# Expert rows gathered by a table from TensorE, outputs scattered to token order, and five places for expert weights in a hybrid encoder layer

## What is computed

```python
x1 = x + merged @ w_out
h = rmsnorm(x1, ffn_norm_g)
g_idx = argmax(h @ w_group_router + b_group_router)        # one of 4 groups, weight g_w
e_logit = (h @ w_expert_router + b_expert_router)[group g_idx]   # 8 experts
top_p, top_i = top_k(softmax(e_logit), 2)
expert_id = g_idx * 8 + top_i
hid = silu(h @ w_exp_gate[e]) * (h @ w_exp_up[e])          # 1024 -> 256
y = x1 + sum over the two chosen e of g_w * top_p[e] * (hid @ w_exp_down[e])
```

## Time and profile before

| | us |
|---|---|
| three runs | 1710.51, 1710.72, 1713.13 |
| median | 1710.72 |
| profiled run | 1707.65 |
| its span | 1706.0 |
| TensorE busy | 1521.2 (89%) |
| VectorE busy | 534.1 (31%) |
| DMA, mean over the span | 148 GB/s |

### The profile page before, as it was taken

How to read it: one execution, slowest core, us unless ns; L and a number is a source line. 1 busy time by engine, 2 the same in 40 slices (tenths; PEclk the granted TensorE clock), 3 DMA queues, 4 the chain that set the end, 5 groups by cost and what they waited for, 6 DMA issues and landing times.

```text
span 1706.0 us, 16754 instructions
## 1 busy us (share of the span) xinstructions
PE 1521.2 (89%) x6566; PEld 841.4 (49%) x6566; DVE 534.1 (31%) x1484; ACT 295.3 (17%) x682; POOL 120.9 (7%) x191
## 2 busy tenths in 40 slices
PE   5999999998799999978999999999999929787870
PEld 3554655445455544455555444765554615444440
DVE  2215598016300033442001344244661521010103
ACT  3224111223101011243000011434000201101100
POOL 6000000112000000000000100100000020000003
PEclk9999999999899999999999999999999859989886
DMA  7332345201521335143114140220132368999995
GB/s 200 126 85 84 94 154 122 82 18 50 156 79 49 123 107 189 50 148 149 50 49 148 50 129 1 75 87 25 50 107 107 120 262 336 422 422 421 422 392 197
DMA packets 132553, 253.15 MB, mean 148 GB/s; under 512 B 11136, under 2 KB 88960, under 8 KB 118144
## 3 DMA queue, kind: packets, MB, share of 16 engines
q1 hardware_dynamic: 115536, 183.55, 30.4%
q0 software_dynamic: 16944, 68.60, 11.2%
HBM read 214.21 MB, written 37.91 MB: 148 GB/s over the span
## 4 chain that ended last, share of the span: by engine, by line
PE 77%; DMA 13%; DVE 4%; issue 2%; ACT 2%; POOL 1%; SPq 1%; DVEq 0%; ACTq 0%; POOLq 0%
PE ps L679 18%; DMA arena<-slot_rows 10%; PE ps L698 7%; PE ps L600 7%; PE ps L610 6%; PE ps L1131 4%; PE ps L649 3%; PE ps L559 3%; PE ps L629 3%; PE ps L1195 2%; PE ps L601 2%; PE ps L611 2%; PE ps L699 2%; PE ps L721 1%; PE ps L1174 1%
## 5 line engine op out<-in xcount | busy, mean ns | idle before, releaser
L679 PE MATMUL ps<-bulk 128*128 128x512 f32 x688 | 303.4, 598 | 2.3 <-issue 2.3
L679 PEld LDWEIGHTS ps<-bulk 128*128 128x128 f32 x688 | 129.8, 192 | 155.8 <-issue 155.8
L600 PE MATMUL ps<-bulk 128*128 128x512 f32 x256 | 133.3, 603 | 4.1 <-DMA bulk<-in_w_in 4.1
L698 PE MATMUL ps<-bulk 128*128 128x512 f32 x256 | 135.2, 610 | 0.0
L610 PE MATMUL ps<-arena,bulk 128*128 128x512 f32 x256 | 131.2, 595 | 1.8 <-DVE arena L1739 1.8
L1174 PE MATMUL ps<-bulk,arena 128*64 128x256 f32 x1024 | 115.8, 385 | 5.4 <-DMA bulk<-in_w_exp_gate 4.7
L1174 PEld LDWEIGHTS ps<-bulk,arena 128*64 128x64 f32 x1024 | 81.5, 139 | 45.7 <-issue 18.3
L1195 PE MATMUL ps<-bulk,arena 128*64 128x512 f32 x256 | 75.9, 747 | 10.9 <-ACT arena L1591 10.9
L601 PEld LDWEIGHTS ps<-bulk 128*128 128x128 f32 x256 | 49.4, 193 | 62.2 <-issue 62.2
L699 PEld LDWEIGHTS ps<-bulk 128*128 128x128 f32 x256 | 48.8, 191 | 61.1 <-issue 61.1
L1161 PE MATMUL ps<-cst,arena 128*128 128x128 f32 x128 | 20.2, 309 | 65.8 <-DMA arena<-slot_rows 65.8
(11 more groups left out here) (376 smaller groups left out, 1987.2 us busy)
## 6 DMA issues: line engine op xcount, KB each, us to landing
bulk<-in_w_exp_gate SPq DMA_DIRECT2D x32, 1024.0 KB, 22.5
bulk<-in_w_exp_up SPq DMA_DIRECT2D x32, 1024.0 KB, 24.6
bulk<-in_w_exp_down SPq DMA_DIRECT2D x32, 1024.0 KB, 22.8
bulk<-in_w_in SPq DMA_DIRECT2D x48, 512.0 KB, 5.1
bulk<-in_w_in SPq DMA_DIRECT2D x7, 2048.0 KB, 10.1
slot_rows<-arena POOLq DMA_DIRECT2D x17, 768.0 KB, 5.9
bulk<-in_w_mem_kv SPq DMA_DIRECT2D x4, 2048.0 KB, 9.4
arena<-slot_rows SPq DMA_DIRECT2D x16, 512.0 KB, 26.1
```

What stands on the lines that cost most here:

```text
L600: mm(ps[4 * q + 1][:, 0:TP], tw[2 * q][:, k, :], hT[:, k, 0:TP], start=k == 0, stop=k == KD - 1)
L679: last = mm(ps[4 + n % 2][:, :], lhs[:, k, tok:tok + P], ring[f % 2][:, k, :], start=k == 0, stop=k == KD - 1)
L698: mm(ps[b][:, 0:TP], tw[s][:, k, :], hT[:, k, 0:TP], start=k == 0, stop=k == KD - 1)
```

## The change

Four things change, in the mixture and ahead of it.

1. *Rows are gathered, not scattered.* `h2` is stored in token order to `h2_rows` by five plain transfers of GpSimd, a tile at a time; `h2` has two places instead of five. For each slot of an expert the kernel needs the number of the pair that owns it. TensorE makes this table: `at_row` (128 tokens x 64) is 1 where the slot within the expert is the token's rank, `at_exp` (128 x 32) holds the pair's number plus one at its expert, and their product, summed over the five tiles and both choices, is the pair number plus one of every slot (20 matmuls into `ps[7]`). `tables` turns it into `put` (the pair's number) and `take` (the token's, half of it). An empty slot becomes a number beyond the tensor. GpSimd gathers each pair's 128 rows with `take`, with a bound, so that numbers out of range are left out.
2. *Results are scattered to token order.* Each pair's results are scattered by `put` into `y_rows`, where both results of a token lie side by side. At the end one plain transfer per tile, issued by SyncE, brings both; SyncE also stores the output tiles.
3. *Five places for weights*, each made of three pieces of 8 KB per partition in `bulk` and `arena`. SyncE loads expert by expert. Experts 0 to 2 and gate of 3 are issued when the merge is over and `x` has come, the rest of 3 after the first fill of `w_out` has been used, expert 4 after the second.
4. The zero fill is gone. Overflow slots get their own table (`at_over`, 10 matmuls after the first `gate_up`). The overflow computation follows behind the first table on VectorE.

To make room, `x1` is built in place over `x`, and the router's tables and the mixture's small tiles move to `work_all` and `mix`.

The diff, cut to its core:

```diff
-        EW = 3 * KD * DF
-        NES = 4
+        EW = KD * DF
+        NES = 5
...
+        places = [[(bulk, 0), (bulk, 8), (bulk, 16)], [(bulk, 80), (bulk, 88), (arena, 40)],
+                  [(arena, 48), (arena, 56), (arena, 64)], [(arena, 72), (bulk, 64), (bulk, 72)],
+                  [(bulk, 48), (bulk, 56), (bulk, 40)]]
...
-            load_gate_up(0)
-            load_down(0)
-            sp.wait_ge(x1_ok, 2 * NT)
-            for e in (1, 2):
-                load_gate_up(e)
+            sp.wait_ge(xr_in, 48)
+            for q in range(2):
+                sp.wait_ge(m_prod[q], 4 * 2 + 1 + 4)
+            for e in range(3):
+                load_gate(e)
+                load_up(e)
                 load_down(e)
-            sp.wait_ge(pos_ok, 2)
-            load_gate_up(3)
+            load_gate(3)
+            sp.wait_ge(n_full, last_item[11] + 1)
+            load_up(3)
             load_down(3)
-            sp.wait_ge(scat, 32 * NT)
-            for n in range(3):
-                load_rows(n)
-            for n in range(2, NPAIR):
-                if n >= 3:
-                    sp.wait_ge(hsT_full, 2 * (n - 2))
-                    load_rows(n)
-                sp.wait_ge(gu_full, n - 1)
-                for e in (2 * n, 2 * n + 1):
-                    load_gate_up(e)
-                sp.wait_ge(dn_full, 2 * (n - 1))
-                for e in (2 * n, 2 * n + 1):
-                    load_down(e)
+            sp.wait_ge(n_full, last_item[12] + 1)
+            load_gate(4)
+            load_up(4)
+            load_down(4)
+            for e in range(NES, NE):
+                n = (e - NES) // 2
+                sp.wait_ge(gu_full, n + 1)
+                load_gate(e)
+                load_up(e)
+                sp.wait_ge(dn_full, 2 * (n + 1))
+                load_down(e)
...
+            for t in range(NT):
+                sp.dma_start(yg[t], y_rows[t * 2 * P:(t + 1) * 2 * P, :].rearrange("(p j) d -> p (j d)", j=2)).then_inc(yg_in[t], 16)
+            for t in range(NT):
+                sp.wait_ge(yg_used, t + 1)
+                dst = o["y_s"].rearrange("b t d -> (b t) d") if t == NTP else o["y_p"][0, t * P:(t + 1) * P, :]
+                sp.dma_start(dst, x1[:, t, :]).then_inc(out_done, 16)
...
+            def pairs_at(t):
+
+                for j in range(2):
+                    for h in range(2):
+                        last = mm(ps[7][h * CAP:(h + 1) * CAP, 0:NPAIR], at_row[:, j, t, :],
+                                  at_exp[:, j, t, :].rearrange("p (n h) -> p h n", h=2)[:, h, :],
+                                  start=(t, j) == (0, 0), stop=(t, j) == (NT - 1, 1))
+                return last
+
+            pe.wait_ge(row_ok, 1)
+            for t in range(NT - 1):
+                pairs_at(t)
+            pe.wait_ge(row_ok, 2)
+            pairs_at(NT - 1).then_inc(take_full, 1)
...
             for n in range(NPAIR):
                 gate_up(n)
+                if n == 0:
+                    pairs_over()
...
+                if t >= 2:
+                    dve.wait_ge(h2T_full, 2 * (t - 1))
+                    dve.wait_ge(rows_out[t % 2], ROWS_OUT[t % 2] + 16 * (t // 2))
...
+            def marked_at(t0, t1):
+
+                for j, hot in enumerate((hot0, hot1)):
+                    h = hot[:, t0:t1, :]
+                    link(v.tensor_tensor(r_tmp[:, t0:t1, :], h, rank_of(t0, t1), ALU.mult))
+                    link(v.tensor_reduce(rank_f[:, j, t0:t1], r_tmp[:, t0:t1, :], AX_X, ALU.add))
+                    last = v.tensor_tensor(at_row[:, j, t0:t1, :], iota_r.unsqueeze(1).to_broadcast([P, t1 - t0, CAP]),
+                                           rank_f[:, j, t0:t1].unsqueeze(2).to_broadcast([P, t1 - t0, CAP]), ALU.is_equal)
+                last.then_inc(row_ok, 1)
+
+            def tables(src, c0, c1):
+
+                w = src.shape[0]
+                t = rt[0:w, 5 * NT * NE:5 * NT * NE + c1 - c0]
+                link(v.tensor_scalar(t, src, 0.0, far[0:w, :], ALU.is_equal, ALU.mult))
+                link(v.scalar_tensor_tensor(t, t, -1.0, src, ALU.add, ALU.add))
+                link(v.tensor_copy(put[0:w, c0:c1], t))
+                return v.tensor_scalar(take[0:w, c0:c1], put[0:w, c0:c1], 1, None, ALU.logical_shift_right)
+
+            for j, hot in enumerate((hot0, hot1)):
+                v.tensor_tensor(at_exp[:, j, :, :], hot, per(pair_id[:, j, :], NE), ALU.mult)
+            dve.wait_ge(rank_full, 1)
+            marked_at(0, NT - 1)
+            dve.wait_ge(rank_full, 2)
+            marked_at(NT - 1, NT)
...
+            dve.wait_ge(take_full, 1)
+            tables(ps[7][:, 0:NPAIR], 0, NPAIR).then_inc(pos_ok, 1)
...
-            for t in range(NT):
-                for j in range(2):
-                    g.indirect_dma_start(slot_rows, bass.IndirectOffsetOnAxis(ap=rows[:, t, j:j + 1].bitcast(U32), axis=0),
-                                         h2[:, t, :], None).then_inc(scat, 16)
...
+            for t in range(NT):
+                pool.wait_ge(h2_ok, t + 1)
+                g.dma_start(h2_rows[t * P:(t + 1) * P, :], h2[t % 2]).then_inc(rows_out[t % 2], 16)
...
+            def take_rows(n):
+                g.indirect_dma_start(hs[n % 3], None, h2_rows, at(take, n, P), bounds_check=T - 1, oob_is_err=False)\
+                 .then_inc(rows_in[n % 3], 16)
...
+            for n in range(3):
+                take_rows(n)
             for n in range(NPAIR):
+                if n + 3 < NPAIR:
+                    pool.wait_ge(hsT_full, 2 * (n + 1))
+                    take_rows(n + 3)
                 pool.wait_ge(ysl_ok, 2 * (n + 1))
-                g.dma_start(slot_rows[n * P:(n + 1) * P, :], ysl[n % 2]).then_inc(ysl_out[n % 2], 16)
+                g.indirect_dma_start(y_rows, at(put, n, P), ysl[n % 2], None, bounds_check=2 * T - 1, oob_is_err=False)\
+                 .then_inc(ysl_out[n % 2], 16)
...
-            for t in range(NT):
-                for j in range(2):
-                    g.indirect_dma_start(yg[t][j], None, slot_rows,
-                                         bass.IndirectOffsetOnAxis(ap=rows[:, t, j:j + 1].bitcast(U32), axis=0)).then_inc(yg_in[t], 16)
```

More of the change, by code:

```diff
@@ L1116, in router_logits @@
                 for k in range(KD):
-                    last = mm(lt_bank(t), h2T[:, k, t * P:(t + 1) * P], w_rt[:, k, :], start=k == 0, stop=k == KD - 1)
+                    last = mm(lt_bank(t), h2T[t % 2][:, k, :], w_rt[:, k, :], start=k == 0, stop=k == KD - 1)
                 if t >= NT - 2:
@@ L1143, in _, with pairs_over @@
                 for s in range(t + 1):
[L1144 removed]
+                    last = mm(rank[:, t * NE:(t + 1) * NE], before if s == t else ones, hot_both[:, s, :], start=s == 0, stop=s == t)
+            last.then_inc(rank_full, 1)
             pe.wait_ge(rt_step, 2)
             t = NT - 1
[L1147 to L1151 removed]
+            mm(ps[4][:, 0:NE], ones, hot_sum, start=True, stop=False)
+            mm(ps[4][:, 0:NE], before, hot_both[:, t, :], start=False, stop=True)
+            mm(ps[4][:, NE:2 * NE], ones, hot_sum, start=True, stop=False)
+            mm(ps[4][:, NE:2 * NE], ones, hot_both[:, t, :], start=False, stop=True).then_inc(rank_full, 1)
+            def pairs_at(t):
[10 more added lines that the diff above has]
+            pairs_at(NT - 1).then_inc(take_full, 1)
+            def pairs_over():
+                pe.wait_ge(row_ok, 3)
+                for t in range(NT):
+                    for j in range(2):
+                        last = mm(ps[5][0:CAP, 0:N_OVER], at_row[:, j, t, :], at_over[:, j, t, :],
+                                  start=(t, j) == (0, 0), stop=(t, j) == (NT - 1, 1))
+                last.then_inc(take_full, 1)
             def rows_transposed(n):
@@ L1168, in gate_up @@
                 pe.wait_ge(hsT_ok, 2 * (n + 1))
-                for c, w, landed in ((0, ew_gate, gate_in[s]), (DF, ew_up, up_in[s])):
-                    pe.wait_ge(landed, 32 * (n // 2 + 1))
+                for c, w, table in ((0, ew_gate, gate_in), (DF, ew_up, up_in)):
+                    for j in range(2):
+                        pe.wait_ge(*landed(table, 2 * n + j))
                     for k in range(KD):
@@ L1187, in down @@
                 pe.wait_ge(hidT_ok, n + 1)
-                pe.wait_ge(down_in[s], 32 * (n // 2 + 1))
+                for j in range(2):
+                    pe.wait_ge(*landed(down_in, 2 * n + j))
                 for c in range(2):
@@ L1219, in _ @@
                     pe.wait_ge(hsT_ok, i * 2 + 2 * (NPAIR + 1))
-                    for c, w, landed in ((0, ew_gate, gate_in[0]), (DF, ew_up, up_in[0])):
-                        pe.wait_ge(landed, i * 16 + (16 * NPAIR + 16))
+                    for c, w, table in ((0, ew_gate, gate_in), (DF, ew_up, up_in)):
+                        pe.wait_ge(table[0][0], i * 16 + landed(table, OVER_E)[1])
                         for k in range(KD):
```

(9 more changed lines are left out.)

230 lines of the change are left out of this document (119 added, 111 removed).

## The result

| | before, us | after, us |
|---|---|---|
| median | 1710.72 (1710.51 to 1713.13, 4 runs) | 1668.09 (1662.17 to 1670.28, 4 runs) |
| profiled run | 1707.65 | 1668.23 |
| its span | 1706.0 | 1666.5 |

The changed kernel is faster: the ratio is 0.9742, with a 95% interval of 0.9716 to 0.9769. Routing ended 3.4 us later in this profiled run than in that of before, through the program ahead of it, so a part of what the start shows is chance.

A forecast was written before the change was run, and what follows sets the result against it. It took matmuls to bound most of the program, and a stop plus DMA bytes its end; terms -20.7, +2.4, -7.5, -4 and -3 sum to -32.8, span 1706.0 to 1673.2, median 1678 us, range 1664 to 1691.

The forecast's parts named there:

- What bounds the kernel: Mostly TensorE's matmuls; near the end a 33.12 us stop before the first pair, then DMA bytes in the expert loop.
- The start: Before the expert loop: a table and gather replace ten scatters, so the first weight release comes 20.7 us earlier.
- Rival (b): At the loop's start, table hand-overs cost double and the first gather lands slowly: 10 us, giving 1688; chance 0.12.
- The gap: At the first weight release: only one expert's gate and up are released, leaving the engines empty once, +2.4 us.
- One expert less: In the loop: 27 experts loaded after the release instead of 28, saving 3.146 MB at 422 GB/s, 7.5 us.
- Empty slots: In the loop's row and result transfers: leaving empty slots out saves 4 us, bounds -13 to +9.
- the forecast's test for it: In the loop: under 415 GB/s with a pair near 17.1 us would show that engines with full rows set the pace.
- Rival (a): In the loop, empty slots save all their bytes: 9 us more saved, giving 1669; chance 0.25.
- The tail: After the loop: results arrive sooner and five tiles' sums shorten, -3 us; what follows the last sum stays at 10.5 us.
- From the profiled run to the median: Whole program: the profiled run lies 3.07 us under the median, so 1674.9 becomes a forecast of 1678.

The follow-up runs named there:

- late_4: The changed kernel with expert 4 loaded only behind the first `gate_up`, so 28 experts load in the loop again: 1673.10 us, ratio 0.9779 to before.
- all_rows: The changed kernel with empty slots given numbers in range, so every gather and scatter moves all 128 rows: 1677.79 us, ratio 0.9803 to before.
- spread_b: The changed kernel with only the order of ranks within an expert's 64 rows altered (row 8i+j holds rank i+8j): 1676.87 us, ratio 0.9796 to before.
- pool_out: The changed kernel with the five result stores given back to GpSimd, as before the change: 1675.07 us, ratio 0.9798 to before.

## Why the prediction was right where it was, and where not

- **What bounds the kernel** was read rightly: the stop before the first pair, and bytes in the loop. TensorE's 65.8 us behind rows went, but in the loop they came back under gate's name, as the prediction said.
- **The start, -20.7: -20.6 measured, which is luck.** Routing ended 3.4 us later in this run, a matter of the program ahead of it, and the two terms behind it were 3.4 us too long. From routing's end to the first gather it was 6.7 us instead of 8.7: the table matmuls took 2.32 us, not 4.5. I had taken the duration of line 1144's although those have 32 columns and 128x128 weights, these 16 and 128x64. My count was off too: the trace has two records for each such matmul of the program (20 at line 1144 for ten, 40 at line 1183 for the twenty of the table), so a record took 0.06 us where I had 0.22 for a whole matmul. And the first rows reached TensorE 4.3 us after the gather's start, where I had 5.7. Rival (b) falls.
- **The gap, +2.4: 1.8 by the issue times, 1.4 by the engines' busy share.** Right in kind, a little over-sized.
- **One expert less, -7.5: between 3 and 6 by late_4.** Over-sized, as far as these runs tell: bytes over rate holds for the transfers, but late_4 also fills the gap; what takes the rest isn't shown.
- **Empty slots, -4 with bounds of -13 and +9: 6.5 by all_rows.** Under-sized. The mechanism was right: the bytes vanish and the engine with the full rows sets the pace. Of the forecast's test for it, under 415 GB/s in the middle of the loop with a pair near 17.1 us, one half showed: a pair took 17.1 us (eight pairs between the gate loads at 1464.54 and 1601.19), but at 420 GB/s. In this kernel the imbalance shows in the last 20 us; only spread_b fell to 412. Rival (a) falls by the same runs: had all saved bytes counted, the three rank orders would have run alike. With the expert's term the two errors cancel, hence -9.7 for -9.1, which is luck again.
- **The tail, -3 with bounds of 0 to -5: -9.2.** This is the step that failed, in its last sentence: what follows the last sum stays. It went from 10.5 to 4.0 us from the last store's issue, since SyncE and no longer GpSimd finishes last. The diff showed that move. The trace of before has the 10.5 us, and in it the last store lands after 3.3, so 7.2 us had no cover by any transfer and should have been asked after. The other terms were near: 8.9 instead of 10 us to the first sum, but 15.1 instead of 13.3 us for the five tiles, since the last load of results took 15.17 us to land and the plain loads came no closer together than the gathers had.
- **From the profiled run to the median, +3.07: -0.1.** The profiled run of before lay 3 us below the median of the others; that of after lay in the middle. Of the 9.9 us between forecast and result, 6.2 are the tail's, 0.6 the loop's, and 3.2 are this, less 0.1 of the start.

## What to carry to other kernels

Where indirect transfers leave rows out, the time falls by what the busiest DMA engine saves, so deal the used rows over the partitions as the engines are dealt; here one table of constants was worth 6.5 us of the loop. When the end of a program has more time behind its last store than a store takes to land, look which engine's program waits for it, and try another than GpSimd. A sum of terms can come out right with wrong terms: read each against its own piece of the trace before trusting the next.

## What the runs showed of the hardware that I had not expected

- An entry out of range moves no row and has no price that shows; gathers and scatters are issued in 1.0 us each. It seems to leave a small packet: from 1270 us on, 6240 packets are under 512 B in after and 4832 in all_rows. Of the latter 128 belong to the eight filling stores, at 16 for a plain store (in before, from 1668 to 1673.5 us), so 1536 are gone, as many as there are empty entries in the sixteen gathers and sixteen scatters.
- Where GpSimd waits for the last store, the execution ends 10.1 to 10.5 us after the store's issue and 6.9 to 7.2 after its landing; where SyncE alone does, 3.0 to 4.0 and 0.4.
- The same 160 projection matmuls took 594 ns each in some runs and 606 in others, here in before and after:

```profile
L1131 PE MATMUL ps<-bulk 128*128 128x512 f32 x160 | 70.1, 595 | 2.1 <-issue 2.1
```
```profile
L1157 PE MATMUL ps<-bulk 128*128 128x512 f32 x160 | 71.8, 606 | 2.1 <-issue 2.1
```

  The early loads aren't the cause: pool_out has them too (0.97 busy DMA engines from 1284 to 1310 us) and took 594. It is the granted clock. The same stretch just behind the projection's first matmul, in before and in after:

```profile
1275.00:1280.00 5.00, 5.00 (x13) 2.15 (x12) 0.00 (x0) 0.00 (x0) 0.00 (x0) 1.00 0.93 314
...
1275.00:1280.00 5.00, 4.82 (x8) 2.07 (x9) 0.00 (x0) 0.00 (x0) 0.01 (x1) 0.66 0.87 248
```

  In after the clock was at the lower of its two levels, 1.2 GHz (0.50 from 1276 to 1279 us), and then back at 1.00; 5 us at 0.66 lose 1.7 us, all of the difference between 70.1 and 71.8. The other six kernels with 606 ns have 0.83 from 1274 to 1284 us, again 1.7 us; the four with 594 ns have 1.00 from 1268 to 1283. TensorE had been idle for 2.06 to 2.07 us just before, at a clock of 1.00, in both groups alike, so why the clock fell in one only is open. This is 1.7 of the 3.4 us by which routing came late; the rest was there before the projection began (1275.18 instead of 1273.43 us).
